# First pass of gated linear attention: second decay and exponential buffers, modulation work between key steps, keys made on VectorE

## The chip, the cores and the metric

One core of a Trainium2 chip. The metric is the device time of one execution in microseconds (us). TensorE multiplies matrices, VectorE and ScalarE work element by element (ScalarE with tables for exponential and logarithm), GpSimd (POOL in the rows) works element by element too and issues gathers, SyncE (SP) issues DMAs.

## What is computed

One layer of a trunk on 128 context tokens and 1024 latent tokens of width 1024, in float32. What matters here, from the reference:

```
m = silu(cond) @ w_ada + b_ada                       # six modulation rows per conditioning vector
h = rms_norm(x, norm_mix) * (1 + sc1) + sh1
la = log_sigmoid(lr @ w_gate + b_gate) / 16          # one decay per head, column and direction
# gated linear attention, both directions, 4 heads, keys of 64, values of 128:
cum = cumsum(la)
o = (q * exp(cum)) @ S  +  (scores of q, k with exp(cum_i - cum_j), masked) @ v
S = exp(last) * S + (k * exp(last - cum)).T @ v
# then attention over keys with cached context keys and values, the output projection,
# and a mixture of 32 experts on all tokens
```

## The kernel before, in words

The program is a row of stages. A stage is one block in which each engine has its own list of instructions, in order, with semaphores between the lists; the next stage begins when all five lists have ended. Tokens go in 9 tiles of 128 (tile 0 is the context, 1 to 8 the latents). The stages are: the first modulation rows; the input projection; gated linear attention (L595 to L990, the stage the change is in); softmax attention (from L1008); output projection and router; and the experts, which take most of the time.

The gated-linear-attention stage has two passes over the nine tiles, `for i in range(NT)` and then `for s in range(NT)`. The first pass takes tiles in the order `FIRST`. For step i, with g = FIRST[i]:

- `gates(i)` (PE, L884): decay logits of the tile, into one of four PSUM banks; issued four steps ahead. `size` (ACT, L676, L677) and `log` (ACT, L681): absolute value, exponential and logarithm; the logarithm needs another table than the exponential, so three tiles' logarithms go together (an ACT_TABLE_LOAD before and after).
- `decay(i)` (DVE, L794 to L806): log-sigmoid, cumulative sum along the tile, differences `Dt` against the tile's middle, and twelve small columns `vecs`.
- `grow(i)` (ACT, L687, L689, L690): `ek` and `eq`, the exponentials of minus and plus `Dt`, and that of the small columns.
- `decayed(i)` (POOL, L757, L760, L762): keys times `ek` for both directions (`kf`, 512 columns), then queries times `eq` for the backward direction (written over the keys) and for the forward one.
- `turn(i)` (PE, L893): four transposes of the decayed keys. `keep_turned(i)` (ACT, L695) copies them from PSUM. `sums(i)` (PE, L903): keys times values, the tile's part of the state. `add(i)` (DVE, L812) takes it to `UX`. `step(k)` (DVE, L822): one tile's state in one direction, sixteen in all.

Between these stands the work on the other modulation rows: eight pieces of `w_ada`, 2 MB each, in a ring of two buffers that SyncE fills (`load`, L629). `ada_part(n)` (PE, L913) multiplies a piece, `ada_keep(n)` (ACT, L700) copies the partial sums, `ada_sum(n)` (PE, L921, L922) adds them and the bias, `ada_row(n)` (ACT, L708) copies the row out, or `ada_scaled(n)` (DVE, L829) for pieces 4 and 5. `ADA_AT` says which steps have a piece (i = 1, 2, 4, 5, 7, 8), and `ADA_LATE` puts pieces 6 and 7 into the second pass. In the kernel before, TensorE's order in a step is gates, turn, sums, ada_sum of the last piece, ada_part of this one.

The second pass, tile g = SECOND[s]: `score` (PE, L931), `mask` (DVE, L835, L837), `centred` (POOL, L770), `mix` (PE, L947, L951), `square` (ACT, L714), `mean` and `gated` (DVE, L841, L848), and GpSimd's power at L781. SyncE's list, in order: constants and states, two modulation pieces, the zeroing of the experts' sums (L650, L652), the new states, then pieces and rows in turn, a piece's load waiting for the product that used its buffer last.

In the softmax-attention stage SyncE first issues the cached keys and values (L1013, L1014), and TensorE begins by transposing the cached keys (L1140), which waits for them; then come the scores of the context tile (L1145).

Of the kernel before, what the change touches and what calls it, by code (L numbers as in the profile page):

```python
# [16 lines left out]
P = 128  # L17
# [17 lines left out]
def trunk_kernel(nc, t_in, t_out):  # L35
# [52 lines left out]
    with ctx:  # L88
# [97 lines left out]
        pre, Dt, ek, eq, kTM, part = (ar(40320 + H * i, H) for i in range(6))  # L186
        nrow2 = ar(43392, H, 2)
        mrow2 = [ar(43904 + H * i, H, 2) for i in range(2)]
        brow2 = [ar(44928 + H * i, H, 1) for i in range(2)]
        sc = [[ar(45952 + 2 * H * i + H * half, H) for half in range(2)] for i in range(2)]  # L190
        sc_both = [ar(45952 + 2 * H * i, 2 * H) for i in range(2)]
        Sc = [r3(ar(48000 + H * i, H), 4) for i in range(2)]
        seen = ar(49024, H).bitcast(I32)
        zeros, osq = ar(49536, P), ar(50700, H)
        keep = ar(50180, H)
        scP = ar(49920, 32 * KT)
        sel = ar(50176, 2)
# [7 lines left out]
        kc = r3(ar(50816, NC * P), NC)  # L205
# [409 lines left out]
        with stage("pads_out") as block:  # L615
            @block.sync
            def _(sp):
# [41 lines left out]
                for n in range(2, NADA):  # L659
                    load(n)  # L660
                    row_out(n - 2)
                    rows(n)
                row_out(NADA - 2)
# [7 lines left out]
            def _(act):  # L671
# [11 lines left out]
                def grow(i):  # L683
                    g = FIRST[i]
                    act.wait_ge(sem("decay_made"), i + 1)
                    act.wait_ge(sem("kf_made"), i)
                    nc.scalar.activation(ek, Dt, ACT.Exp, scale=-1.0 / 16).then_inc(sem("ek_made"), 1)  # L687
                    act.wait_ge(sem("qf_made"), i)
                    nc.scalar.activation(eq, Dt, ACT.Exp, scale=1.0 / 16).then_inc(sem("eq_made"), 1)  # L689
# [31 lines left out]
                for i in range(NT):  # L721
                    if i % 3 == 0 and i + 3 < NT:
                        size(i + 3)
                        size(i + 4)
                    grow(i)
                    if i % 3 == 1 and i + 2 < NT:
                        size(i + 4)
                    keep_turned(i)
                    if i % 3 == 1 and i + 2 < NT:
                        for k in range(i + 2, i + 5):  # L730
                            log(k)
                    if i - 1 in ADA_AT:
                        ada_row(ADA_AT[i - 1])
                    if i in ADA_AT:
                        ada_keep(ADA_AT[i])
                ada_row(ADA_AT[NT - 1])
# [8 lines left out]
            def _(pool):  # L745
# [18 lines left out]
                def centred(s):  # L764
                    g = SECOND[s]
# [1240 lines left out]
```

## Time and profile before, and how to read it

| | |
|---|---|
| median of 3 runs | 2820.37 us (2819.17 to 2822.82) |
| the profiled execution | 2821.45 us, span 2819.8 us |
| busy over the span | PE 88%, DVE 58%, ACT 47%, POOL 30% |
| gated-linear-attention stage | about 419.7 to 584.5 us |
| its first pass, first to ninth transpose | 435.22 to 519.54 us |
| DMA | 539.95 MB, 191 GB/s over the span |

Times in rows are microseconds from the start of the span. A row of a timeline gives start, duration, engine, line, operation, result and source with their sizes, how many follow one another, and in brackets the engine's idle time before it and what ended it. PE is TensorE's matmul, PEld its weight load; a float32 product counts as two or more instructions. PEclk is the clock granted to TensorE, 1.00 for 2.4 GHz and 0.50 for 1.2 GHz.

### The profile page before, as it was taken

To read this page: it belongs to the slowest core of one execution; us is meant where nothing else is said; L and a number is where in the kernel's file an instruction comes from. 1 tells how busy PE (TensorE), PEld (TensorE's weight loads), DVE (VectorE), ACT (ScalarE), POOL (GpSimd) and SP (SyncE) were. 2 spreads that over 40 slices of the span, in tenths; PEclk is the share of its full clock that TensorE was granted. 3 is DMA by queue.
4 is the path that set the end of the run, shared out by engine and by line. 5 is a ranking of instruction groups with operands and counts; after the bars stand their busy time and mean duration, and the time that the engine had idled before them with its cause. 6 is when DMAs were issued, how large, how long until landed. Compare 5 with 4: busy or idle time off the path is not lost. (4 is left out here: it accounts for less than half of the span.)

```text
span 2819.8 us, 55873 instructions
## 1 busy us (share of the span) xinstructions
PE 2484.2 (88%) x19085; PEld 1367.2 (48%) x19086; DVE 1625.0 (58%) x1900; ACT 1322.4 (47%) x1351; POOL 833.6 (30%) x862
## 2 busy tenths in 40 slices
PE   4999986879999983989989999689998999998992
PEld 0555543456665542545545555345554455544551
DVE  1222215457774554595483567999869835256895
ACT  0111115235442223584482566888768725155771
POOL 3121122210000334333332343333344333233342
PEclk8999995789999986989989999899999999999996
DMA  8000007230003227787485678899979946158984
GB/s 329 27 9 17 17 6 241 91 109 1 0 0 121 90 83 259 228 326 280 119 327 173 204 243 289 329 398 394 368 257 369 356 128 209 30 147 291 340 305 151
DMA packets 176502, 539.95 MB, mean 191 GB/s; under 512 B 20644, under 2 KB 36438, under 8 KB 175380
## 3 DMA queue, kind: packets, MB, share of 16 engines
q1 hardware_dynamic: 146240, 488.92, 46.4%
q0 software_dynamic: 26720, 46.85, 7.7%
q10 hardware_dynamic: 3496, 3.61, 0.4%
q8 instruction: 24, 0.39, 0.1%
q14 instruction: 22, 0.18, 0.0%
HBM read 494.69 MB, written 45.21 MB: 191 GB/s over the span
## 5 line engine op out<-in xcount | busy, mean ns | idle before, releaser
L1910 PE MATMUL psum<-arena 128*64 128x512 bf16 x12528 | 1436.3, 386 | 98.9 <-DVE arena L1805 91.8
L1910 PEld LDWEIGHTS psum<-arena 128*64 128x64 bf16 x12528 | 727.2, 111 | 755.4 <-DVE arena L1805 115.8
L1805 DVE TENSOR_TENSOR arena<-arena 128x2048 bf16<-128x2048 f32 x384 | 858.1, 2285 | 179.8 <-ACT arena L1707 152.4
L1707 ACT ACTIVATE arena<-arena 128x2048 bf16<-128x2048 f32 x384 | 706.5, 1899 | 42.7 <-PE psum L1910 20.5
L1660 POOL DMA_INDIRECT expert_sums<-arena x90 | 186.3, 2071 | 540.2 <-issue 521.1
L559 PE MATMUL psum<-arena 128*128 128x512 f32 (+2 forms) x864 | 305.8, 511 | 1.2 <-issue 1.2
L1640 POOL DMA_INDIRECT arena<-expert_inputs,arena x88 | 130.1, 1478 | 484.7 <-DMA arena<-expert_lists 419.6
L559 PEld LDWEIGHTS psum<-arena 128*128 128x128 f32 x864 | 152.3, 193 | 133.1 <-issue 129.8
L1809 DVE TENSOR_TENSOR arena<-psum,arena 128x512 bf16<-128x512 f32 x87 | 59.6, 686 | 212.7 <-ACT arena L1717 212.7
L1728 ACT ACTIVATE arena<-psum,arena 128x512 f32<-128x512 f32 x87 | 59.7, 686 | 205.4 <-PE psum L1910 153.3
L1713 ACT ACTIVATE arena<-psum 128x1024 bf16<-128x1024 bf16 x87 | 88.5, 1018 | 125.1 <-PE psum L1910 118.7
L1671 POOL DMA_DIRECT2D arena<-expert_lists x174 | 130.2, 941 | 30.9 <-issue 25.6
L1723 ACT ACTIVATE arena<-arena 128x512 f32<-128x512 f32 x87 | 54.9, 631 | 174.0 <-DVE arena L1813 174.0
L1492 PE MATMUL psum<-arena 128*128 128x512 f32 x288 | 128.8, 601 | 1.4 <-DVE arena L1390 1.4
L1823 DVE TENSOR_SCALAR arena<-psum 128x512 f32<-128x512 f32 x87 | 59.9, 689 | 108.4 <-PE psum L1910 101.6
L1192 PE MATMUL psum<-arena 128*128 128x128 f32 x640 | 105.4, 288 | 6.1 <-ACT arena L1055 2.9
L1717 ACT ACTIVATE arena<-psum 128x512 bf16<-128x512 f32 x87 | 51.6, 593 | 122.6 <-PE psum L1894 122.1
L1899 PE MATMUL psum<-arena 128*64 128x512 bf16 x522 | 103.1, 390 | 3.4 <-DMA arena<-bias_parts 2.8
L1201 PE MATMUL psum<-arena 128*64 128x128 f32 x1280 | 96.8, 282 | 0.0
L1063 ACT ACTIVATE arena<-psum 128x512 f32<-128x512 f32 x64 | 38.1, 597 | 115.8 <-PE psum L1192 115.8
L1888 PE MATMUL psum<-arena 128*128 128x128 bf16 x704 | 54.5, 221 | 41.7 <-DMA arena<-expert_inputs,arena 41.7
L1043 ACT ACTIVATE arena<-psum,arena 128x1280 f32<-128x1280 f32 x64 | 85.0, 1328 | 8.5 <-DVE arena L1093 1.3
(246 smaller groups left out, 2294.5 us busy)
## 6 DMA issues: line engine op xcount, KB each, us to landing
arena<-in_w_gu SPq DMA_DIRECT2D x256, 1024.0 KB
arena<-in_w_down SPq DMA_DIRECT2D x128, 1024.0 KB, 6.7
arena<-in_w_ada SPq DMA_DIRECT2D x12, 2048.0 KB, 10.3
arena<-in_w_in SPq DMA_DIRECT2D x8, 1168.0 KB, 20.5
arena<-in_x_sample SPq DMA_DIRECT2D x16, 512.0 KB
arena<-mod_rows SPq DMA_DIRECT2D x12, 512.0 KB, 7.3
expert_sums<-arena SPq DMA_DIRECT2D x10, 512.0 KB, 6.2
expert_inputs<-arena SPq DMA_DIRECT2D x10, 512.0 KB, 2.8
```

The costliest lines, as they stand in the source:

```text
L559: last = nc.tensor.matmul(bank(bk, n, off), hT[b][:, j * P:(j + 1) * P], w_in[:, j, lo:lo + n], start=(j == 0), stop=(j == KT - 1))
L1192: last = nc.tensor.transpose(bank(t_bank(r - 1, i), P, at * P), pr[(r - 1) % 2][:, v * KEYS + k * P:v * KEYS + (k + 1) * P], ident)
L1201: last = nc.tensor.matmul(bank(O_BANK)[heads_rows(v), q * P:(q + 1) * P], va[:, 1 + k, v * HD:(v + 1) * HD], pT[r % 2][:, v * KEYS + k * P ...
L1492: last = nc.tensor.matmul(bank(a), mixT[b][:, j * P:(j + 1) * P], w_out[:, j, a * H:(a + 1) * H], start=(j == 0), stop=(j == KT - 1))
L1640: pool.indirect_dma_start(out=xg, out_offset=None, in_=h2_d, in_offset=bass.IndirectOffsetOnAxis(ap=listed.bitcast(U32)[:, 0:1], axis=0)). ...
L1660: pool.indirect_dma_start(out=moe_halves, out_offset=bass.IndirectOffsetOnAxis(ap=held.bitcast(U32)[:, 2 * DELAY:2 * DELAY + 1], axis=0), ...
L1671: pool.dma_start(listed[group(h), :], pairs[:, h, :]).then_inc(sem("listed_in"), 16)
L1707: nc.scalar.activation(w_hi[c], raw[c], ACT.Copy).then_inc(sem(f"hi_made{c}"), 1)
L1713: nc.scalar.activation(xT, bank(B_X).bitcast(BF), ACT.Copy).then_inc(sem("xT_made"), 1)
L1805: nc.vector.tensor_tensor(w_lo[c], raw[c], w_hi[c], ALU.subtract).then_inc(sem(f"lo_made{c}"), 1)
L1899: nc.tensor.matmul(bank(b)[group(g)], pickrow[:, (first + g) * UNIT:(first + g + 1) * UNIT], rows, start=True, stop=False)
L1910: last = nc.tensor.matmul(bank(b)[group(g)], parts[part][:, cols], w[:, kk, g * H:(g + 1) * H], start=False, stop=(k == KT - 1 and part == 1))
```

## The change

In five parts, of which the last moves work from the stage behind into this one:

- `Dt` and `ek` have two buffers each, by the parity of i. `decay(i)` waits for the exponential of two steps back instead of the last, `grow(i)` for the keys of two steps back. The arena's map is laid out anew for it.
- The keys times `ek` are made by VectorE (`decay_keys`), behind the decay of the next tile and ahead of the state add; `add` and `step` each stand one step later in VectorE's list.
- On TensorE `ada_part(n)` stands ahead of `turn(i)` and `ada_sum(n)` between `turn(i)` and `sums(i)` of the same step; `score(0)` stands ahead of the last `turn`. On ScalarE `grow(i)` comes first, then `size` and `log`, `ada_keep`, `keep_turned`, `ada_row`.
- `mask(0)` stands ahead of the last `add`, and GpSimd's `centred` waits for the small columns' exponential.
- The four DMAs of cached keys and values are issued in this stage, ahead of the last two modulation rows, to a new place for the keys.

```
-        pre, Dt, ek, eq, kTM, part = (ar(40320 + H * i, H) for i in range(6))
+        pre, eq, kTM, part = (ar(40320 + H * i, H) for i in range(4))
+        Dt, ek = ([ar(42368 + H * (2 * k + i), H) for i in range(2)] for k in range(2))
...
+                sp.wait_ge(sem("z_made"), NT)
+                for a in range(NC):
+                    sp.dma_start(kc[:, a, :], t_in["cache_k"]...).then_inc(sem("cache_in"), 16)
+                    sp.dma_start(va[:, NT + a, :], t_in["cache_v"]...).then_inc(sem("cache_in"), 16)
                 row_out(NADA - 2)
...
                 def grow(i):
-                    act.wait_ge(sem("kf_made"), i)
-                    nc.scalar.activation(ek, Dt, ACT.Exp, scale=-1.0 / 16).then_inc(sem("ek_made"), 1)
+                    if i >= 2:
+                        act.wait_ge(sem("kf_made"), i - 1)
+                    nc.scalar.activation(ek[i % 2], Dt[i % 2], ACT.Exp, scale=-1.0 / 16).then_inc(sem("ek_made"), 1)
                     act.wait_ge(sem("qf_made"), i)
...
                 for i in range(NT):
-                    if i % 3 == 0 and i + 3 < NT:
+                    grow(i)
+                    if i + 3 < NT and i % 3 == 0:
                         size(i + 3)
                         size(i + 4)
-                    grow(i)
-                    if i % 3 == 1 and i + 2 < NT:
+                    if i + 4 < NT and i % 3 == 1:
                         size(i + 4)
-                    keep_turned(i)
-                    if i % 3 == 1 and i + 2 < NT:
                         for k in range(i + 2, i + 5):
                             log(k)
-                    if i - 1 in ADA_AT:
-                        ada_row(ADA_AT[i - 1])
                     if i in ADA_AT:
                         ada_keep(ADA_AT[i])
-                ada_row(ADA_AT[NT - 1])
+                    keep_turned(i)
+                    if i in ADA_AT:
+                        ada_row(ADA_AT[i])
...
                 def decayed(i):
-                    pool.wait_ge(sem("ek_made"), i + 1)
-                    nc.gpsimd.tensor_tensor(r4(kf[:, g, :]), k_tile(g).unsqueeze(1).broadcast_to([P, 2, 2, P]), r4(ek), ALU.mult).then_inc(sem("kf_made"), 1)
...
                 def centred(s):
+                    pool.wait_ge(sem("vecs_made"), FIRST.index(g) + 1)
...
                 def decay(i):
-                    dve.wait_ge(sem("eq_made"), i)
+                    if i >= 2:
+                        dve.wait_ge(sem("eq_made"), i - 1)
...
+                def decay_keys(i):
+                    g = FIRST[i]
+                    dve.wait_ge(sem("ek_made"), i + 1)
+                    nc.vector.tensor_tensor(r4(kf[:, g, :]), k_tile(g).unsqueeze(1).broadcast_to([P, 2, 2, P]), r4(ek[i % 2]), ALU.mult).then_inc(sem("kf_made"), 1)
...
                 for i in range(NT):
                     if i + 1 < NT:
                         decay(i + 1)
-                    add(i)
-                    if i == 1:
+                    decay_keys(i)
+                    if i >= 1:
+                        add(i - 1)
+                    if i == 3:
                         dve.wait_ge(sem("state_in"), 64)
-                    if i >= 2:
-                        step(i - 2)
+                    if i >= 3:
+                        step(i - 3)
...
-                step(NT - 2)
                 dve.wait_ge(sem("sc_cleared"), 2)
                 dve.wait_ge(sem("seen_in"), 16)
                 mask(0)
-                for k in range(NT - 1, len(STEPS)):
+                step(NT - 3)
+                add(NT - 1)
+                for k in range(NT - 2, len(STEPS)):
                     step(k)
...
                     if i + 4 < NT:
                         gates(i + 4)
-                    turn(i)
-                    sums(i)
-                    if i - 1 in ADA_AT:
-                        ada_sum(ADA_AT[i - 1])
                     if i in ADA_AT:
                         ada_part(ADA_AT[i])
-                pe.wait_ge(sem("decay_logged"), NT)
-                score(0)
-                ada_sum(ADA_AT[NT - 1])
+                    if i == NT - 1:
+                        score(0)
+                    turn(i)
+                    if i in ADA_AT:
+                        ada_sum(ADA_AT[i])
+                    sums(i)
```

TensorE, steps i = 7 and 8 of the first pass and the begin of the second, before. L893 is a transpose group, L903 the state sums, L921 and L922 a modulation sum, L913 a modulation product, L931 a score group:

```order
L893 MATMUL psum<-arena 128x128 x4
L903 MATMUL psum<-arena 64x128 x8
L913 MATMUL psum<-arena 32x512 x8
L893 MATMUL psum<-arena 128x128 x4
L903 MATMUL psum<-arena 64x128 x8
L921 MATMUL psum<-arena 2x512
L922 MATMUL psum<-arena 2x512
L913 MATMUL psum<-arena 32x512 x8
L931 MATMUL psum<-arena 128x128 x8
L921 MATMUL psum<-arena 2x512
L922 MATMUL psum<-arena 2x512
L931 MATMUL psum<-arena 128x128 x8
```

The same two steps with the change, where L904 is the transpose group, L914 the state sums, L932 and L933 the modulation sum, L924 the product and L942 the score group:

```order
L924 MATMUL psum<-arena 32x512 x8
L904 MATMUL psum<-arena 128x128 x4
L932 MATMUL psum<-arena 2x512
L933 MATMUL psum<-arena 2x512
L914 MATMUL psum<-arena 64x128 x8
L924 MATMUL psum<-arena 32x512 x8
L942 MATMUL psum<-arena 128x128 x8
L904 MATMUL psum<-arena 128x128 x4
L932 MATMUL psum<-arena 2x512
L933 MATMUL psum<-arena 2x512
L914 MATMUL psum<-arena 64x128 x8
L942 MATMUL psum<-arena 128x128 x8
```

The product went from behind the step's state sums to ahead of its transposes, the modulation sum from the step after to between transposes and state sums, and the first score from behind the last product to ahead of the last transposes.

VectorE, step i = 3 of the first pass, before. L794 to L806 are the decay of tile i + 1, L812 the state add, L822 a state step:

```order
L794 SCALAR_TENSOR_TENSOR arena<-psum,arena 128x512
L796 SCALAR_TENSOR_TENSOR arena<-arena 128x512
L797 TENSOR_TENSOR arena<-arena 128x256
L800 TENSOR_TENSOR arena<-arena 128x256
...
L806 TENSOR_TENSOR arena<-arena 128x2
L812 TENSOR_TENSOR arena<-psum,arena 128x512
L822 SCALAR_TENSOR_TENSOR arena<-arena 128x128 x2
```

And with the change (L814 is the key product, L820 the add, L830 the step):

```order
L795 SCALAR_TENSOR_TENSOR arena<-psum,arena 128x512
L797 SCALAR_TENSOR_TENSOR arena<-arena 128x512
L798 TENSOR_TENSOR arena<-arena 128x256
L803 TENSOR_TENSOR arena<-arena 128x256
...
L809 TENSOR_TENSOR arena<-arena 128x2
L814 TENSOR_TENSOR arena<-arena 128x512
L820 TENSOR_TENSOR arena<-psum,arena 128x512
L830 SCALAR_TENSOR_TENSOR arena<-arena 128x128 x2
```

The key product is new on VectorE, between the next tile's decay and the add, and the add is now that of the step before.

## Rows read from the trace of the kernel before

**Rows 1.** Busy time by stretch: PE, PEld, DVE, ACT, POOL, then PEclk, DMA share, GB/s.

```profile
435.20:477.40 42.20, 32.09 (x152) 16.47 (x152) 22.81 (x50) 17.65 (x32) 11.94 (x12) 0.58 0.83 262
477.40:519.50 42.10, 27.62 (x136) 11.44 (x136) 21.88 (x49) 15.06 (x28) 11.13 (x12) 0.62 0.29 101
...
536.40:584.50 48.10, 41.57 (x408) 31.54 (x408) 22.10 (x70) 12.45 (x76) 17.20 (x23) 1.00 0.08 30
```

**Rows 2.** Waits from 434 to 530 (us in total, times, longest).

```profile
POOL arena L757 <- ACT arena L687: 71.1, 9, 12.1
...
PE psum L893 <- POOL arena L757: 22.7, 8, 4.0
```

**Rows 3.** Timeline of TensorE, step i = 5 and the next transposes.

```profile
487.69 1.12 PE L893 MATMUL psum<-arena 128*128 128x128 f32 x4 [4.01 <-POOL arena L757]
489.49 1.98 PE L903 MATMUL psum<-arena 128*64 128x128 f32 x16 [0.69 <-ACT arena L695]
...
494.05 3.30 PE L913 MATMUL psum<-arena 128*32 128x512 f32 x13
499.95 0.90 PE L893 MATMUL psum<-arena 128*128 128x128 f32 x3 [2.60 <-POOL arena L757]
```

**Rows 4.** Timelines of ScalarE and GpSimd, the same stretch.

```profile
495.09 0.59 ACT L708 ACTIVATE arena<-psum 2x512 f32<-2x512 f32 x1 [5.65 <-PE psum L922]
...
497.93 0.62 ACT L687 ACTIVATE arena<-arena 128x512 f32<-128x512 f32 x1
...
498.63 1.27 POOL L757 TENSOR_TENSOR arena<-arena 128x512 f32<-128x512 f32 x1 [9.26 <-ACT arena L687]
```

**Rows 5.** Timeline of TensorE, first, fifth and ninth transposes of the pass.

```profile
435.22 1.11 PE L893 MATMUL psum<-arena 128*128 128x128 f32 x4 [3.65 <-POOL arena L757]
...
477.42 1.12 PE L893 MATMUL psum<-arena 128*128 128x128 f32 x4 [0.54 <-POOL arena L757]
...
519.54 0.74 PE L893 MATMUL psum<-arena 128*128 128x128 f32 x4 [2.59 <-POOL arena L757]
```

**Rows 6.** Timeline of VectorE, a decay's begin, the next one's, and an add.

```profile
428.69 0.69 DVE L794 SCALAR_TENSOR_TENSOR arena<-psum,arena 128x512 f32<-128x512 f32 x1 [13.61 <-ACT arena L681]
...
432.17 0.68 DVE L794 SCALAR_TENSOR_TENSOR arena<-psum,arena 128x512 f32<-128x512 f32 x1
...
491.51 0.69 DVE L812 TENSOR_TENSOR arena<-psum,arena 128x512 f32<-128x512 f32 x1 [1.84 <-PE psum L903]
```

**Rows 7.** Timeline of TensorE at either clock, and busy time of one stretch.

```profile
438.92 2.07 PE L884 MATMUL psum<-arena 33*128 33x128 f32 x8
...
532.06 1.02 PE L922 MATMUL psum<-arena 128*2 128x512 f32 x2
...
542.24 1.92 PE L913 MATMUL psum<-arena 128*32 128x512 f32 x16
...
516.50:520.00 3.50, 0.91 (x8) 0.42 (x4) 0.00 (x0) 1.75 (x4) 1.64 (x2) 0.99 0.00 0
```

**Rows 8.** Timeline of VectorE, from the first mask to the second.

```profile
532.62 3.23 DVE L822 SCALAR_TENSOR_TENSOR arena<-arena 128x128 f32<-128x128 f32 x12
...
536.42 1.31 DVE L837 COPY_PREDICATED arena<-arena,psum 128x512 f32<-128x512 int32 x2
```

**Rows 9.** One line's instructions, ns min/median/max, first and last start.

```profile
L800 DVE TENSOR_TENSOR arena<-arena x9: 424/1000/1006, 431.1 to 509.1; 128x256 f32<-128x256 f32 x9
```

**Rows 10.** Timeline of SyncE's queue, and DMA issues from 455 to 475.

```profile
456.59 0.59 SPq L629 DMA_DIRECT2D arena<-in_w_ada  x1
...
arena<-in_w_ada SPq DMA_DIRECT2D x2, 2048.0 KB, 7.8
```

**Rows 11.** Timeline, begin of the softmax-attention stage.

```profile
588.10 0.36 SPq L1013 DMA_DIRECT2D arena<-in_cache_k  x1
...
591.33 0.69 PE L1140 MATMUL psum<-arena 128*128 128x128 f32 x2 [10.46 <-DMA arena<-in_cache_v]
```

**Rows 12.** The page's DMA issues (KB each, median us to landing).

```profile
arena<-in_w_in SPq DMA_DIRECT2D x8, 1168.0 KB, 20.5
```

More of the change, by code:

```diff
@@ L185, in trunk_kernel @@
         RING_B = [r3(ar(32128 + 4096 * i, 4096), KT) for i in range(2)]
-        pre, Dt, ek, eq, kTM, part = (ar(40320 + H * i, H) for i in range(6))
[L187 to L197, printed above, removed]
+        pre, eq, kTM, part = (ar(40320 + H * i, H) for i in range(4))
+        Dt, ek = ([ar(42368 + H * (2 * k + i), H) for i in range(2)] for k in range(2))
+        nrow2 = ar(44416, H, 2)
+        mrow2 = [ar(44928 + H * i, H, 2) for i in range(2)]
+        brow2 = [ar(45952 + H * i, H, 1) for i in range(2)]
+        sc = [[ar(46976 + 2 * H * i + H * half, H) for half in range(2)] for i in range(2)]
+        sc_both = [ar(46976 + 2 * H * i, 2 * H) for i in range(2)]
+        Sc = [r3(ar(49024 + H * i, H), 4) for i in range(2)]
+        seen = ar(50048, H).bitcast(I32)
+        zeros, scP, sel, keep = ar(50560, P), ar(50688, 32 * KT), ar(50944, 2), ar(50948, H)
+        osq = ar(40320, H)
         oattT = r3(ar(36224, 4 * TOK), 4)
@@ L204, in trunk_kernel @@
         mx3, mx2, c_sum, c_share = ar(25472, 3), ar(25475, 2), ar(25477, NH), ar(25485, NH)
-        kc = r3(ar(50816, NC * P), NC)
+        kc = r3(ar(51460, NC * P), NC)
         w_out = r3(ar(27008, KT * DM), KT)
@@ L613, in trunk_kernel @@
         u4 = lambda ap: ap.rearrange("p (u t) -> p u t", u=4)
-        with stage("pads_out") as block:
+        with stage("pads_out cache_in") as block:
             @block.sync
@@ L662, in _ @@
                     rows(n)
+                sp.wait_ge(sem("z_made"), NT)
+                for a in range(NC):
+                    sp.dma_start(kc[:, a, :], t_in["cache_k"][0, 0, a * P:(a + 1) * P].rearrange("s h d -> s (h d)")).then_inc(sem("cache_in"), 16)
+                    sp.dma_start(va[:, NT + a, :], t_in["cache_v"][0, 0, a * P:(a + 1) * P].rearrange("s h d -> s (h d)")).then_inc(sem("cache_in"), 16)
                 row_out(NADA - 2)
@@ L685, in grow @@
                     act.wait_ge(sem("decay_made"), i + 1)
-                    act.wait_ge(sem("kf_made"), i)
-                    nc.scalar.activation(ek, Dt, ACT.Exp, scale=-1.0 / 16).then_inc(sem("ek_made"), 1)
+                    if i >= 2:
+                        act.wait_ge(sem("kf_made"), i - 1)
+                    nc.scalar.activation(ek[i % 2], Dt[i % 2], ACT.Exp, scale=-1.0 / 16).then_inc(sem("ek_made"), 1)
                     act.wait_ge(sem("qf_made"), i)
-                    nc.scalar.activation(eq, Dt, ACT.Exp, scale=1.0 / 16).then_inc(sem("eq_made"), 1)
+                    nc.scalar.activation(eq, Dt[i % 2], ACT.Exp, scale=1.0 / 16).then_inc(sem("eq_made"), 1)
                     nc.scalar.activation(vecs[:, :, :, g], vecs[:, :, :, g], ACT.Exp, scale=1.0 / 16).then_inc(sem("vecs_made"), 1)
@@ L798, in decay @@
                     last, c_f, c_b = col(p4, P - 1), col(p4[:, 0:2], mid - 1), col(l4[:, 2:4], mid)
-                    dve.wait_ge(sem("eq_made"), i)
-                    nc.vector.tensor_tensor(r4(Dt)[:, 0], p4[:, 0:2], bc(c_f, P), ALU.subtract)
-                    nc.vector.tensor_tensor(r4(Dt)[:, 1], bc(c_b, P), l4[:, 2:4], ALU.subtract)
+                    if i >= 2:
+                        dve.wait_ge(sem("eq_made"), i - 1)
+                    to = r4(Dt[i % 2])
+                    nc.vector.tensor_tensor(to[:, 0], p4[:, 0:2], bc(c_f, P), ALU.subtract)
+                    nc.vector.tensor_tensor(to[:, 1], bc(c_b, P), l4[:, 2:4], ALU.subtract)
                     nc.vector.tensor_copy(vecs[:, 0, :, g], last)
@@ L1010, in _ @@
             def _(sp):
-                for a in range(NC):
-                    sp.dma_start(kc[:, a, :], t_in["cache_k"][0, 0, a * P:(a + 1) * P].rearrange("s h d -> s (h d)")).then_inc(sem("cache_in"), 16)
-                    sp.dma_start(va[:, NT + a, :], t_in["cache_v"][0, 0, a * P:(a + 1) * P].rearrange("s h d -> s (h d)")).then_inc(sem("cache_in"), 16)
                 for c in range(2):
```

## The prediction

> **What bounds the kernel now.** I read the busy times by stretch first. The gated-linear-attention stage is 165 us of 2820. In its first pass, the first two rows of [rows 1], TensorE works 59.7 of 84.3 us and no other engine more than 44.7: no engine is full, so the order of waits sets the time. The granted clock there is 0.58 and 0.62, so the 1.2 GHz level for most of the stretch; in the second pass, the third row, it is 1.00. The waits [rows 2] say who is late: GpSimd waits 71.1 us for ScalarE's exponential, TensorE 22.7 us for GpSimd's keys.
>
> The period from i = 5 to 6 shows the ring [rows 3, 4]. TensorE transposes the keys (487.69), multiplies them into the state sums (489.49), does the modulation sum, which ScalarE takes at 495.09, and the next modulation product (until 497.35). Only then does ScalarE copy that, form the exponential (497.93), and GpSimd multiply the keys (498.63); the next transpose starts at 499.95. The period is 12.26 us, and TensorE idles 2.6 us in front of the transpose. Every modulation piece stands in the ring whole, because ScalarE forms step i+1's exponential behind step i's modulation copy. From the first transpose (435.22) to the ninth (519.54) are 84.3 us [rows 5], 10.5 a period.
>
> **The change, part by part.** (a) *Keys on VectorE.* GpSimd's product takes 1.27 us [rows 4]; the VectorE product of 512 columns nearest to it takes 0.69 (L812) [rows 6]: 0.6 us less in the ring, nine more instructions (about 6 us) on VectorE, which has room. Against it: the first key product now stands behind the second tile's decay. The decay occupies VectorE 3.5 us undisturbed (428.69 to the next at 432.17) [rows 6], so the first product starts at about 435.7; GpSimd's 1.27 us before the transpose at 435.2 began at 433.9; the first transpose moves to about 436.5: +1.3 us.
>
> (b) *Second decay and exponential buffers.* They let the decay and the exponential run a tile ahead. Alone they are worth little: in the period shown the exponential waits for ScalarE's own turn behind the modulation work, not for a buffer. Late next is GpSimd's query product, which the second exponential still waits for; it is 1.5 us a step and hidden. Cost of the buffers themselves: nothing, they are addresses.
>
> (c) *The modulation product ahead of the transpose, the modulation sum ahead of the state sums.* The product needs only weights that have landed, so it runs while ScalarE and VectorE make the keys; the state sums and the next product then run behind the modulation row that ScalarE waits for. The ring that is left is exponential 0.6, keys 0.7, transpose 1.1, modulation sum 3.6, row copy 0.6: 6.9 us with hand-offs at the low clock [rows 3, 4]. TensorE's own list becomes the longer one. Between first and ninth transpose it holds 8 transposes, 8 state sums, 5 modulation sums, 6 products, 4 gate groups and one score. At 1.2 GHz [rows 3, 4, 7]: 8x1.12 + 8x1.98 + 5x3.6 (from the state sums' end to 495.09) + 6x3.3 + 4x2.07 + 2.0 (the score has as many matmuls as the state sums) = 72.9 us. At 2.4 GHz [rows 5, 7]: 8x0.74 + 8x1.2 + 5x2.04 (L921 as L922) + 6x1.92 + 4x1.2 + 1.2 = 43 us. State sums, gates and score at that level have no row here; half their length and all of it bound them, and I take 1.2, nearer to the half, since products and sums go from 3.3 to 1.92 and from 3.6 to 2.04. At the high level VectorE is the longer: 3.5 decay + 0.69 keys + 0.69 add + 0.54 step = 5.4 us a step [rows 6, 8].
>
> (d) *GpSimd beside VectorE.* L800 takes 424 ns alone and 1000 in most steps [rows 9], and it stands in the list where GpSimd multiplies. Before, GpSimd worked 2.8 us a step (11.94 and 11.13 us in four steps each [rows 1]), and L800 alone lost 0.58. Now it works 1.5 us a step, beginning with the add, which reads PSUM, so I take 0.5 to 0.9 us: 5.9 to 6.3 us a step. The Trainium skill ("SBUF — State Buffer", Who interferes with whom) states that a VectorE instruction with two SBUF inputs contends with GpSimd's reads, and one with a single SBUF input does not. The new key product has two SBUF inputs; by that rule it meets only GpSimd's products of the step before, which are over.
>
> (e) *Which clock.* In the trace the clock is at 2.4 GHz right behind a full modulation product, 0.99 at 516.5 to 520.0 [rows 7]. There it is wasted, since TensorE works 0.91 of those 3.5 us. Now transpose and sums stand right behind the product. I take the high level for most of the last half, and one period of four at the low one: one at 1.12 + 1.98 + 3.6 + 3.3 = 10.0, three at 6.3, 7.2 us a period. The Trainium skill ("TensorE: Matmul & The Clock Gate", What's actually happening) says that activity releases the throttle and idling brings it back; the second pass, busy 41.6 of 48.1 us at 1.00 [rows 1], agrees.
>
> (f) *Weights.* The third piece (2 MB) is issued at 456.6, behind the zeroing of the expert sums, and lands 7.8 us later, at 464.4 [rows 10]. The change doesn't move that issue. The fifth transpose (tile step i = 4) now stands behind its product, so it can't start before 464.4 + 1.9; with most of the product at the low clock I take 467.5, against 477.42 [rows 5]. TensorE's list up to that point (4 transposes, 4 state sums, 2 modulation sums, 3 products, 4 gate groups) would end at 436.5 + 37.8 = 474 all low and 459 all high, so 467.5 is also its middle: -9.9 us, with the +1.3 of (a) and ScalarE's logarithm groups of i = 1 and i = 4 inside it (the second runs while the piece is waited for). Pieces 3, 4 and 5 are issued two pieces ahead, some 15 us, and hidden; without that cover each costs up to what a landing exceeds it by.
>
> (g) *Last four periods.* Before 519.54 - 477.42 = 42.1 us, now 4x7.2 = 28.8: -13.3 us.
>
> (h) *End of the first pass.* From the ninth transpose to the second mask (L837, 536.42) were 16.9 us [rows 5, 8]: modulation sum, last product, score and sum stood in between. Now product and score are in front. Left are transpose 0.74, sum 2.0, state sums 1.2, hand-offs 0.2, add 0.6, nine steps of two instructions at 0.27 us (12 took 3.23 [rows 8]) 4.9, scaling 0.6: 10.2 us, so -6.7 us. From there the second pass is as before; its two products have their weights 10 us earlier.
>
> (i) *Cached keys and values.* Now the attention stage issues them at 588.10 and TensorE starts at 591.33 [rows 11]. Issued a stage earlier, TensorE can start at about 588.2: -3.1 us. The four issues (1.6 us of the queue) stand in front of the last two rows, whose sources come much later: nothing.
>
> Sum: -9.9 - 13.3 - 6.7 - 3.1 = -33.0 us. The profiled execution took 2821.45 us (span 2819.8), so 2788.4 for its like; the median of the runs is 2820.37, 1.1 lower: **2787.4 us**. The fast end takes 466.3 in (f), 6.0 a period and 9.8 in (h): -11.1 - 18.1 - 7.1 - 3.1 = -39.4, 2781.0. Later stages lie behind this one and shift with it.
>
> **Rivals.** *The clock stays at 1.2 GHz.* For it: the mean is 0.58 and 0.62 in the first pass [rows 1]. Against it: every full product raised it. Then 436.5 + 72.9 = 509.4 for the ninth transpose, 13.0 us behind it (1.12, 3.6 and 1.98 in (h)): 522.4 against 536.4, with (i) -17.1 us: 2803.3.
>
> *Weights come late.* TensorE now stands still for a late piece before it transposes. If a landing takes 20.5 us, as w_in's do [rows 12], the third piece costs 12.7 us: 2800.1. Against it: 7.8 us in this very stretch.
>
> *VectorE becomes the bound, slower than before.* If GpSimd's lock held all of VectorE's step at L800's ratio, 1.00/0.424 = 2.36, the 5.4 us would be 12.7 a period: +17 us over eight, the nine late steps 6.6 more, which eats (h), with (i) +14: 2834. It decides from some 10.9 us a period, twice the undisturbed 5.4. Against it: GpSimd works only 1.5 us a step.
>
> *The gain is given back.* The second pass waits for the last two modulation rows or pieces, and a few us remain: 2817. Nothing in its rows shows such a wait.
>
> **How the numbers follow.** Forecast 0.68 (2780 to 2797), clock low 0.19, weights late 0.06, given back 0.03, lock 0.04. A measurement tells 0.2% (5.6 us) from no change. Faster by more takes the first three: 0.93; within 0.03; slower 0.04. The range 2780 to 2806 holds the forecast and the low clock with 2 us of slack, and leaves out the ends.
>
> **What would show it.** Transposes some 7 us apart with the fifth near 467; the second mask near 504; granted clock over 0.8 in the last half of the pass; GpSimd's products 1.5 us a step; L800's like mostly 0.42 us; no wait of TensorE at the attention stage's start. It is wrong if TensorE waits for weights after the third piece, if the clock stays at 0.5, or if periods stay over 9 us.

## The result and the profile after

| | us |
|---|---|
| before, median of 4 runs (the three above and one beside the change) | 2820.30 (2819.17 to 2822.82) |
| after, median of 4 runs | 2780.57 (2778.91 to 2782.44) |
| ratio | 0.9858, 95% interval 0.9841 to 0.9875 |
| profiled execution, before and after | 2821.45, 2780.45 (span 2778.8) |

The kernel got faster by 1.4%, 39.7 us between the medians, where -33.0 was forecast. The time 2780.57 lies just inside the range, 0.6 us above its low end; that it fell inside is in part luck, since four executions of the same kernel later ran from 2777.10 to 2783.32 (experiment 12).

The stretches come first, with the columns of [rows 1]: first to fifth transpose, fifth to ninth, second pass.

```profile
434.90:468.80 33.90, 27.85 (x168) 14.45 (x168) 24.44 (x57) 21.07 (x37) 8.07 (x10) 0.70 1.00 315
468.80:493.30 24.50, 20.81 (x160) 8.64 (x156) 17.37 (x44) 11.78 (x23) 5.81 (x8) 0.93 0.49 174
502.00:549.00 47.00, 41.56 (x408) 31.54 (x408) 21.02 (x67) 11.53 (x69) 17.16 (x23) 1.00 0.10 33
```

The two halves took 42.2 and 42.1 us and take 33.9 and 24.5. The granted clock rose from 0.58 and 0.62 to 0.70 and 0.93. The second pass is what it was. The waits from 434 to 502 answer to [rows 2]:

```profile
POOL arena L760 <- DVE arena L814: 55.6, 9, 14.3
...
PE psum L904 <- DVE arena L814: 7.6, 3, 4.8
DVE arena L814 <- ACT arena L691: 7.3, 3, 4.6
```

TensorE waits 7.6 us for keys instead of 22.7. GpSimd's 55.6 us of waiting cost nothing. Below, TensorE from the third modulation piece on (i = 4 to 7), to be read beside [rows 3]:

```profile
465.54 3.40 PE L924 MATMUL psum<-arena 128*32 128x512 f32 x16 [2.78 <-DMA arena<-in_w_ada]
468.87 0.66 PE L904 MATMUL psum<-arena 128*128 128x128 f32 x4
469.66 1.02 PE L932 MATMUL psum<-arena 1*2 1x512 f32 x2
470.61 1.02 PE L933 MATMUL psum<-arena 128*2 128x512 f32 x2
471.56 1.09 PE L914 MATMUL psum<-arena 128*64 128x128 f32 x16
472.58 1.92 PE L924 MATMUL psum<-arena 128*32 128x512 f32 x16
474.97 0.66 PE L904 MATMUL psum<-arena 128*128 128x128 f32 x4 [0.47 <-DVE arena L814]
...
480.86 0.66 PE L904 MATMUL psum<-arena 128*128 128x128 f32 x4 [2.31 <-DVE arena L814]
482.20 1.98 PE L914 MATMUL psum<-arena 128*64 128x128 f32 x16 [0.69 <-ACT arena L699]
484.11 2.65 PE L924 MATMUL psum<-arena 128*32 128x512 f32 x16
486.75 0.66 PE L904 MATMUL psum<-arena 128*128 128x128 f32 x4
```

From 465.54 to 474.50 product, transposes, modulation sum, state sums and the next product stand almost without a gap. At 2.4 GHz each takes little over half of its time at the low level in [rows 3, 7]. The periods from fifth to ninth transpose are 6.10, 5.89, 5.89 and 6.60 us. At 480.86 TensorE has waited 2.31 us for VectorE's keys, so its own work doesn't set that period. VectorE has no gap in the next, in which the clock fell for the state sums (1.98):

```profile
474.23 0.69 DVE L814 TENSOR_TENSOR arena<-arena 128x512 f32<-128x512 f32 x1 [4.64 <-ACT arena L691]
...
480.12 0.68 DVE L814 TENSOR_TENSOR arena<-arena 128x512 f32<-128x512 f32 x1
480.72 0.68 DVE L820 TENSOR_TENSOR arena<-psum,arena 128x512 f32<-128x512 f32 x1
481.32 1.30 DVE L830 SCALAR_TENSOR_TENSOR arena<-arena 128x128 f32<-128x128 f32 x2
482.55 0.68 DVE L795 SCALAR_TENSOR_TENSOR arena<-psum,arena 128x512 f32<-128x512 f32 x1
...
486.01 0.68 DVE L814 TENSOR_TENSOR arena<-arena 128x512 f32<-128x512 f32 x1
```

From one key product to the next are 5.89 us: VectorE is the bound there. That holds for the two periods of 5.89 us. In the first of the four (6.10) VectorE's key product, at 474.23, waited 4.64 us for ScalarE's exponential, which stood behind the modulation row's copy and a table load. In the last (6.60) TensorE's list, now with the first score in it, has no gap over 0.1 us from 486.75 to 493.35.

**Where the 41.0 us of the profiled pair are.** I count from the stage's first decay (428.69 before, 427.29 after), so that what lies ahead of the stage drops out:

| us after the first decay | before | after | difference, of this stretch alone |
|---|---|---|---|
| first transpose | 6.53 | 7.68 | +1.15 |
| fifth transpose | 48.73 | 41.58 | -8.30 |
| ninth transpose | 90.85 | 66.06 | -17.64 |
| second mask | 107.73 | 74.75 | -8.19 |
| last gated output of the second pass | 154.69 | 121.69 | -0.02 |
| attention's first transpose | 162.64 | 126.45 | -3.19 |

That makes -36.2. The stage itself began 1.4 us earlier, and the experts' long stretch (first to last start of its main product, L1916 after) took 1672.5 us instead of 1676.4. The change touches neither. The other runs show that the latter is chance (experiment 12), and the stage's first decay stood anywhere from 425.4 to 427.2 us in the twelve kernels run later, so it too varies. Half a microsecond the other way is spread over the rest. What the prediction said would show it is there: transposes 7.3 us apart on the mean, the fifth at 468.87, the second mask at 502.04, the clock over 0.8 in the last half, and no wait for weights after the third piece.

### The profile page after: what moved, and what is told of

The parts are those of the page before. It is cut to its first block and busy times, and to the rows that moved or that the text cites. A ratio compares the mean times of both kernels' runs of the same rounds, so it can differ in the third digit from the quotient of the medians.

```text
span 2778.8 us, 55870 instructions
## 1 busy us (share of the span) xinstructions
PE 2464.0 (89%) x19085; PEld 1360.0 (49%) x19086; DVE 1621.5 (58%) x1909; ACT 1321.6 (48%) x1351; POOL 816.8 (29%) x853
## 5 line engine op out<-in xcount | busy, mean ns | idle before, releaser
L1916 PE MATMUL psum<-arena 128*64 128x512 bf16 x12528 | 1437.2, 386 | 94.6 <-DVE arena L1811 89.1
L1916 PEld LDWEIGHTS psum<-arena 128*64 128x64 bf16 x12528 | 728.3, 112 | 750.6 <-DVE arena L1811 111.6
L1713 ACT ACTIVATE arena<-arena 128x2048 bf16<-128x2048 f32 x384 | 706.4, 1898 | 42.2 <-PE psum L1916 20.0
L1646 POOL DMA_INDIRECT arena<-expert_inputs,arena x88 | 139.0, 1580 | 493.4 <-DMA arena<-expert_lists 427.7
```

What stands on the lines that cost most here:

```text
L1646: pool.indirect_dma_start(out=xg, out_offset=None, in_=h2_d, in_offset=bass.IndirectOffsetOnAxis(ap=listed.bitcast(U32)[:, 0:1], axis=0)). ...
L1713: nc.scalar.activation(w_hi[c], raw[c], ACT.Copy).then_inc(sem(f"hi_made{c}"), 1)
L1916: last = nc.tensor.matmul(bank(b)[group(g)], parts[part][:, cols], w[:, kk, g * H:(g + 1) * H], start=False, stop=(k == KT - 1 and part == 1))
```

## The experiments

"Second mask" below is its time after the first decay: before 107.7, after 74.8 (73.0 when the same kernel ran again, so that a difference of under 2 us there tells nothing). A ratio is to the kernel before, run beside it on the same chip, with its 95% interval; where neither stands, the kernel ran once. Line numbers shift by a line or two between the kernels, so parts go by their names.

**1. The old order with everything else of the change.** TensorE and ScalarE lists as before; keys on VectorE, two buffers and the early cached keys stay.

```
-                    if i in ADA_AT:
-                        ada_part(ADA_AT[i])
                     turn(i)
-                    if i in ADA_AT:
-                        ada_sum(ADA_AT[i])
                     sums(i)
+                    if i - 1 in ADA_AT:
+                        ada_sum(ADA_AT[i - 1])
+                    if i in ADA_AT:
+                        ada_part(ADA_AT[i])
```

> The changed kernel, with the order of the modulation work on TensorE and ScalarE put back as it was before; keys on VectorE, two buffers and the early cached keys stay. If the order makes the gain, the ring keeps every modulation piece: it is shorter than before only by the faster key product (0.6 us in each of 8 periods) and the cached keys (3.2 us), so some 8 us below before, 2812. If keys on VectorE or the buffers make the gain, it stays near the changed kernel, 2781 to 2790.

Measured 2817.67 us (ratio 0.9992, 0.9981 to 1.0002); second mask 106.45. The order carries the gain. Keys, buffers and cache together are not told from nothing in the median, and the 1.3 us at the second mask are less than the same kernel varies by. The trace does have the 3.2 us at the attention stage.

**2. The order alone.** Keys on GpSimd, one buffer, add and step in their old places; new order, early cache.

```
                 def grow(i):
-                    if i >= 2:
-                        act.wait_ge(sem("kf_made"), i - 1)
+                    act.wait_ge(sem("kf_made"), i)
...
                 def decayed(i):
+                    pool.wait_ge(sem("ek_made"), i + 1)
+                    nc.gpsimd.tensor_tensor(r4(kf[:, g, :]), ..., r4(ek[0]), ALU.mult).then_inc(sem("kf_made"), 1)
...
-                    decay_keys(i)
-                    if i >= 1:
-                        add(i - 1)
+                    add(i)
```

> The new order of the modulation work alone (with the early cached keys): keys on GpSimd, one decay and one exponential buffer, adds and steps as before. If the order makes the gain, most of it is here: periods of some 7 to 8 us, 2790. If keys and buffers make it, near 2815.

Measured 2782.27 us (0.9869, 0.9853 to 0.9886); second mask 76.43. The intervals of this ratio and of the change's overlap: new order and early cache give all that can be told.

**3. Keys on GpSimd, two buffers.** `decay_keys` is taken out and the product put back on GpSimd.

> The changed kernel with the key product back on GpSimd (1.27 us instead of 0.69). VectorE bounds the late periods at 5.9 us if the trace is read right; it loses an instruction of 0.6 us and meets GpSimd for 2.8 us a step instead of 1.5, so both sides weigh about the same: 2781 to 2786. If the key product in the ring bounds, 0.6 us in each of 8 periods: 2785.5. If keys on VectorE were what makes the gain, over 2800.

Measured 2782.49 us (0.9871, 0.9852 to 0.9889); second mask 74.26. Moving the keys to VectorE is worth nothing that can be told: it takes 0.6 us out of the hand-off and puts as much into the engine that bounds the late periods.

**4. One buffer.** `Dt` and `ek` single, the waits one step tighter, all else as after.

```
-                    if i >= 2:
-                        dve.wait_ge(sem("eq_made"), i - 1)
+                    dve.wait_ge(sem("eq_made"), i)
```

> The changed kernel with one decay and one exponential buffer. VectorE then waits with each decay's differences until the second exponential of the step before is made, and the key product stands behind that decay: ring of exponentials 1.1, differences and small columns 1.3, keys 0.7, transpose and sum 2.7, row 0.6, 6.4 us a period instead of 5.9 in the late ones and some 1 to 2 us more in the early ones: 2784 to 2790. If the buffers are worth nothing, 2781.

Measured 2785.91 us (0.9879, 0.9862 to 0.9895); second mask 76.90. The longest of its waits that the kernel after does not have, from 434 to 502, is the decay's for the exponential that still reads `Dt`:

```profile
DVE arena L801 <- ACT arena L692: 11.0, 5, 4.3
```

The mask comes 2.2 us later than in the change, 3.9 later than in experiment 12, so its own size is not well known. The four late periods tell more: they sum to 27.1 us, against 24.5 and 24.6 in two executions of the change, so the second buffers are worth 2.6 us there. Up to the fourth transposes another 2.8 us are lost (31.73 us after the first decay for 28.93), but these fall into the wait for the third piece. With keys on GpSimd the two kernels (experiments 2 and 3, mask 76.43 and 74.26) differ in the order of add, step and mask as well, and only 0.5 us of the difference lies in the late periods.

**5. Cached keys late.** The four DMAs back in the attention stage.

> The changed kernel with the four DMAs of cached keys and values back at the start of the attention stage. If TensorE's wait there was the whole of term (i), the stage's first transpose comes 3.2 us later behind the second pass's end (8.0 us instead of 4.8) and nothing else moves: 2783.8. If the first score waits for another engine in either case, no difference.

One run: 2785.13 us. From the last gated output to attention's first transpose are 7.95 us, as before, against 4.76 with the change: 3.2 us, the forecast's 3.1.

**6. The experts' sums zeroed late.** The zeroing DMAs go behind the last piece, so that the third piece is not queued behind them.

```
                 load(0)
                 load(1)
-                sp.wait_ge(sem("zeroed"), 1)
-                for a in range(NT + 1):
-                    sp.dma_start(moe_d[a * P:(a + 1) * P, :]...).then_inc(sem("zeros_out"), 16)
```

> The changed kernel with the zeroing of the expert sums (11 DMAs, 5.8 MB written) issued behind the last modulation piece, in the second pass, where the DMA engines idle. If the third piece's landing held the fifth transpose, the 2.8 us of TensorE's wait go, less what ScalarE's logarithm group then sets (it ends at 467.0, the product would at 466.2): 2 to 3.5 us less in the period of 12.65, 2778. If the logarithm group was the bound in any case, 0 to 0.5 us. If the zeroing is missed later or collides with pieces 6 and 7, slower by some us.

Measured 2785.02 us (0.9873, 0.9856 to 0.9889); second mask 73.38. The wait for the piece is gone (the product starts at 462.58 with no idle time), but the next wait stood right behind it:

```profile
467.46 1.02 PE L932 MATMUL psum<-arena 1*2 1x512 f32 x2 [1.20 <-ACT arena L704]
468.40 1.87 PE L933 MATMUL psum<-arena 128*2 128x512 f32 x2
470.20 1.87 PE L914 MATMUL psum<-arena 128*64 128x128 f32 x16
```

ScalarE copies the partial sums only behind a table load and three logarithms (until 466.9), TensorE waits, and the clock falls during the sums. The next period grew from 6.1 to 8.24 us. Of 3.1 us in the one period 1.4 were left at the mask, no more than the same kernel varies by, and nothing at the end of the second pass (121.91 us after the first decay for 121.69). The 2778 expected did not come. A version with the logarithms elsewhere was not tried; none of the kernels run beats the change.

**7. Keys made twice.** VectorE makes each step's key product once more, into a place nobody reads.

> The changed kernel with a second key product per step on VectorE (into unused space, 0.6 us, ahead of the one that counts). If VectorE bounds the periods from the sixth transpose on, each of these grows from 5.9 to 6.5, and where it doesn't bound nothing: 3 to 5 periods, +2 to +3 us in the pass. If TensorE's list bounds, +0 in those periods.

One run: 2781.94 us; second mask 75.32. The key products of two steps stand 6.49 us apart:

```profile
478.62 0.69 DVE L814 TENSOR_TENSOR arena<-arena 128x512 f32<-128x512 f32 x1
479.22 0.69 DVE L815 TENSOR_TENSOR arena<-arena 128x512 f32<-128x512 f32 x1
...
485.11 0.69 DVE L814 TENSOR_TENSOR arena<-arena 128x512 f32<-128x512 f32 x1
```

5.89 plus 0.60 is 6.49: in the two periods that took 5.89 us VectorE's list is the bound, to a hundredth. The last late period did not grow (6.45 us for 6.60): that one is TensorE's. Up to the fourth transposes the extra work shows too (30.36 us after the first decay for 28.93) and then falls into the wait for the third piece. At the mask the expected +2 to +3 us are 0.6 against the change and 2.4 against its second execution (experiment 12), too uncertain to count.

**8. Each modulation product of the first pass twice.**

> The changed kernel with each of the six modulation products of the first pass made twice on TensorE (same result, 1.92 us at the high clock, 3.4 at the low). TensorE's list in a late period is 0.66 + 2.0 + 1.1 + 1.9 = 5.7 of 5.9 us, so nearly all of it should show: 1.7 us in each late step with a piece, more in the first one: +9 to +12 us in the pass, 2791. If the order of waits bounds and TensorE has slack, under +3.

One run: 2786.98 us; second mask 80.17, 5.4 later (7.2 later than in experiment 12). That lies between the two cases expected. The extra product is 1.7 to 3.0 us of TensorE in each of six steps, some 12 us in all, of which about half is hidden beside the other engines. TensorE has slack beside VectorE, but less than a product.

**9. Only the product ahead of the transposes.** From the kernel after, the modulation sum put behind the state sums.

```
                     turn(i)
+                    sums(i)
                     if i in ADA_AT:
                         ada_sum(ADA_AT[i])
-                    sums(i)
```

> The kernel after, with TensorE's modulation sum put behind the state sums of the same step; the product stays ahead of the transposes, ScalarE's order is the new one. Theory A (the product's place carries the gain, since before it ended last in each step and ScalarE's copy of it stood ahead of the next exponential): the row copy now comes one state sum (1.1 to 2.0 us) later, hidden in part under VectorE's 5.9 us a step; second mask 76 to 80 us after the first decay (74.8 in the kernel after), 2782 to 2788 us. Theory B (the sum has to be ahead of the state sums as well, since ScalarE takes the row before the next exponential): the late periods go to 8 us, second mask 82 to 90, 2789 to 2797 us.

Measured 2786.45 us (0.9883, 0.9867 to 0.9900); second mask 79.00. Both lie in theory A's ranges: with the product ahead and ScalarE's new order, 27.4 of the 31.7 us between experiment 1 and the change are there at the mask, and the sum's place ahead of the state sums adds 4.3. ScalarE's order alone can't be run with TensorE's old one: ScalarE would wait for the product ahead of copying the transposes, and TensorE would wait for that copy ahead of the product.

**10. Only the modulation sum ahead of the state sums.** From experiment 1, the sum of the step before between transposes and state sums; the product stays last.

> The kernel with the old order of modulation work on TensorE and ScalarE, and in it only the modulation sum of the step before moved ahead of the state sums; the product stays last in its step. Theory A (the product's place carries the gain): the ring over the product stays as it was, the row copy only starts 1.1 to 2.0 us earlier while the product behind it still ends last; second mask 103 to 107 us after the first decay (106.5 in the old order), 2813 to 2818 us. Theory B (half of the gain is the sum's): second mask 88 to 98, 2797 to 2808 us.

Measured 2802.10 us (0.9937, 0.9920 to 0.9953); second mask 95.87. Theory A had 103 to 107, theory B 88 to 98: it is B, and theory A falls in this form. The shares of the two moves don't add up (10.6 us for the sum alone here, 4.3 on top of the product in experiment 9), so neither has one price.

**11. TensorE's new order, ScalarE's old one.**

```
                 for i in range(NT):
-                    grow(i)
...
                     keep_turned(i)
...
+                    if i - 1 in ADA_AT:
+                        ada_row(ADA_AT[i - 1])
                     if i in ADA_AT:
                         ada_keep(ADA_AT[i])
-                    keep_turned(i)
-                    if i in ADA_AT:
-                        ada_row(ADA_AT[i])
```

> The kernel after on TensorE, with ScalarE's old order: transposes' copy before the copy of the partial sums, the row copied a step later. Theory A (TensorE's place of the product carries the gain, ScalarE's order little): the modulation sum waits for the transposes' copy and that of the partial sums one behind the other, some 1 us more in a step with a piece, and TensorE has about that slack; second mask 75 to 80 us after the first decay, 2781 to 2788 us. Theory C (ScalarE's order is needed too): TensorE stands still 1.5 us or more in each of the six steps with a piece, second mask 84 to 90, 2790 to 2797 us.

Measured 2802.55 us (0.9938, 0.9921 to 0.9955); second mask 94.40. Theory C, and more: TensorE waits for the copy of the partial sums, which now stands behind the copy of the transposes:

```profile
PE psum L934 <- ACT arena L704: 13.9, 6, 4.1
```

**The orders side by side.** The stretch from first to ninth transpose, with the columns of [rows 1]: experiment 1 (old order), 10 (sum moved), 11 (ScalarE's order old), 9 (sum behind), and after.

```profile
433.04:512.79 79.75, 59.28 (x288) 27.77 (x288) 40.24 (x96) 32.58 (x59) 12.41 (x16) 0.60 0.58 187
```

```profile
433.72:506.43 72.71, 54.64 (x289) 25.59 (x289) 40.07 (x96) 32.58 (x59) 12.40 (x16) 0.68 0.63 205
```

```profile
434.28:511.06 76.78, 58.23 (x324) 26.48 (x324) 40.21 (x99) 31.87 (x59) 13.88 (x18) 0.69 0.60 194
```

```profile
433.07:496.81 63.74, 52.16 (x324) 23.84 (x324) 42.53 (x99) 32.60 (x60) 13.90 (x18) 0.77 0.73 235
```

```profile
434.97:493.35 58.38, 48.71 (x324) 23.09 (x325) 41.74 (x99) 32.85 (x60) 13.88 (x18) 0.80 0.78 255
```

Those with x324 hold 36 instructions more: a product (1.92 us), a score (1.16) and a modulation sum (2.04), which now stand ahead of the ninth transposes. Less those 5.1 us, TensorE's busy time for the same instructions goes from 59.3 (old order) to 43.6 us (after): 15.7 us are the clock. Its idle time (stretch less busy) goes from 20.5 to 9.7: 10.8 us are waits. Experiment 10 shows how both hang together, in the period that [rows 3] show of before:

```profile
481.15 1.11 PE L906 MATMUL psum<-arena 128*128 128x128 f32 x4 [3.40 <-DVE arena L816]
482.20 1.86 PE L934 MATMUL psum<-arena 1*2 1x512 f32 x2
483.99 1.87 PE L935 MATMUL psum<-arena 128*2 128x512 f32 x2
485.79 1.81 PE L916 MATMUL psum<-arena 128*64 128x128 f32 x16
487.53 1.92 PE L926 MATMUL psum<-arena 128*32 128x512 f32 x16
491.41 0.65 PE L906 MATMUL psum<-arena 128*128 128x128 f32 x4 [1.96 <-DVE arena L816]
```

The product still ends last and the ring is the same, yet the period is 10.26 us instead of 12.23 in experiment 1. From the transposes' start to the product's end are 8.3 us; there they were 10.25 (483.22 to 493.47). The modulation sum fills the 0.69 us in which TensorE waited for ScalarE's copy of the transposes, and the product that follows runs at 2.4 GHz, 1.92 us for all 16 instructions, where [rows 3] show 3.30 for 13 of them. That the filled gap is what raised the clock is argued from these rows; no run filled it with idle work alone. Such a gap doesn't always come with the low level: in experiments 11 and 12 state sums behind a gap of 0.69 us took 1.09 us, the time at 2.4 GHz (at 496.29 and at 479.27).

**12. The kernel after, once more.**

> The kernel after once more, to see what varies between builds and executions of the same code. If the 3.9 us by which the experts' stage of the profiled execution after was shorter than before is chance, this one's experts' stage lies anywhere in 1672 to 1680 us (the eight kernels so far span 1672.5 to 1679.3), and its median in 2778 to 2787 us; if the change brings it, the stage is 1672.5 within 0.5 us. Second mask at 74.8 within 0.3 us after the first decay either way.

Measured 2782.27 us (2777.10 to 2783.32; 0.9868, 0.9851 to 0.9884). The experts' stretch took 1674.7 us, and the stage's first decay stood at 426.00. Over all the kernels here, whose code there is the same, it took 1672.5 to 1679.3, so the 3.9 us of the first pair are chance. I expected the second mask within 0.3 us of 74.8, and it came at 72.97: the product on the third piece started at 36.1 us after the first decay instead of 38.3, since the piece landed 8.4 us behind its issue and not 10.2. The second pass took 48.5 us instead of 46.9 and gave most of that back, see the last section.

## Why the prediction was right

The direction and the mechanism held. The sum was 3.2 us short up to the attention stage's first transpose (-36.2 for -33.0): two terms were too small by 4.3 and 1.5 us, and one was too large by 2.8, so errors cancelled in part. What lies outside, mostly chance, added the rest.

- **(a)** held. First transpose +1.15 us, forecast +1.3; the product takes 0.68. But it brings nothing on the whole (experiment 3).
- **(b)** "They are worth little" held for the old order (experiment 1); the sum gave them nothing in the new one as well, and there it was wrong by 2 us or more (experiment 4). Once the wait for ScalarE's turn was gone, the buffer's came up.
- **(c)** The order is the gain: experiments 1 and 2. What I had not priced apart is ScalarE's half. With TensorE's new order alone (experiment 11) 20 us are lost. And I took the gain for one of who waits for whom, with the clock as an extra; by experiment 10 a third of it (10.6 of 31.7 us at the second mask) comes with the product still last in its step.
- **(d)** held where VectorE is the bound, in two of the four late periods: 5.89 us, forecast 5.9 to 6.3. The price fell on other instructions: the decay's L803, which is L800 of [rows 9], is now undisturbed, and the two instructions of the state step take 1.30 us instead of 0.60, +0.70.

```profile
L803 DVE TENSOR_TENSOR arena<-arena x9: 424/424/426, 429.7 to 485.0; 128x256 f32<-128x256 f32 x9
```

- **(e)** is the step that failed most. I charged one late period of four at the low clock, 10.0 us. There was one such stretch (the state sums at 482.20 took 1.98, the product 2.65), and it cost nothing, since VectorE was the bound of that period. The four took 6.10, 5.89, 5.89 and 6.60 us, 6.1 on the mean for the 7.2 forecast. Besides, the 3.3 us taken for a product at the low level, here and in the rival of the low clock, is 13 of its 16 instructions in [rows 3]; a whole one took 3.64 us at 440.68.
- **(g)** is the sum of it: -17.64 for -13.3.
- **(f)** was too large: -7.15 for -9.9 (-9.04 in experiment 12). "The change doesn't move that issue" was true of the third piece, 28.0 us after the first decay in both. But the fourth piece was issued 6.1 us behind it before (462.70) and now 1.4 us behind it (456.69), because the product that frees its buffer ends sooner; the two 2 MB loads now overlap. The issues at 455.25 and at 456.69:

```profile
arena<-in_w_ada SPq DMA_DIRECT2D x1, 2048.0 KB, 10.2
...
arena<-in_w_ada SPq DMA_DIRECT2D x1, 2048.0 KB, 14.0
```

  The landing took 10.2 us and not 7.8, which is most of the 2.8 us missing. It is the weak form of the rival *Weights come late*; experiment 6, with the piece there in time, ended the second pass no sooner. That the fourth load held the third up is not shown. In the nine runs that issue the two 1.4 us apart the third took 8.2 to 10.2 us, and with the fourth 4.7 us or more behind it 7.9 to 8.3 (before, experiments 1, 10 and 11). But pieces 6 and 7, issued 1.2 us apart in the second pass of the kernel after, took 7.8 and 13.3: there the first of the pair lost nothing.
- **(h)** -8.19 for -6.7. Behind the last add stood seven state steps (3.76 us for 14 instructions), not nine (4.9 us). The loop that ends the pass does run from the eighth step to the last, but `STEPS` has seven pairs, fourteen steps and not the sixteen counted at the head of this document.
- **(i)** held: -3.19 for -3.1; TensorE starts behind the stage's boundary and waits for no DMA.

```profile
553.74 0.66 PE L1146 MATMUL psum<-arena 128*128 128x128 f32 x2 [7.26 <-PEq L107]
```

Of the rivals, *the clock stays at 1.2 GHz* didn't come: 0.80 over the pass. *VectorE becomes the bound* came, but at 5.89 us and not at 10.9. *The gain is given back* didn't: the second pass takes 47.0 us in both.

By the Trainium skill ("SBUF — State Buffer", Who interferes with whom), cited in (d), a VectorE instruction with two SBUF inputs contends with a GpSimd instruction that reads SBUF, and one with a single SBUF input does not. The trace agrees: the add, one of whose inputs is in PSUM, keeps its 0.68 us at 480.72 while GpSimd starts a product at 480.95, and the state step behind it, with SBUF inputs alone, takes 1.30 us for 0.60.

## What to carry to other kernels

When one engine works on two jobs, put what another engine waits for early and fill the hand-offs with the second job, and reorder the lists of both engines together: TensorE's new order without ScalarE's gave 15 of 37 us. A gap can cost more than its length: of the 26.5 us that the same work got shorter between the first and the ninth transposes, 15.7 are a higher clock and 10.8 shorter waits. And where a faster loop frees a buffer sooner, ask beside which transfer the next load will now run: the second of two loads issued 1.4 us apart landed after 14.0 us for 7.7 before. Here it was still early enough.

## What was not expected of the hardware

- The same kernel's second pass took 46.9 us in one execution and 48.5 in another. In the slower, TensorE's score behind the 2.63 us of idling before the second pass ran at the low level: 1.77 us for 1.16, and the next two rows too (1.13 for 0.64, 1.74 for 1.16). First the kernel after, then experiment 12:

```profile
503.49 1.16 PE L942 MATMUL psum<-arena 64*128 64x128 f32 x16 [2.63 <-DVE arena L845]
```

```profile
500.42 1.77 PE L942 MATMUL psum<-arena 64*128 64x128 f32 x16 [2.63 <-DVE arena L845]
```

  The idling is as long in both, and the clock fell in one and not in the other. So it is with the state sums behind the fourth transposes: behind 1.90 us of idling in either execution they took 1.98 us at 458.78 and 1.09 at 457.48. Experiment 6 met the lower level ahead of its second pass too (1.62 us, second pass 48.5). Differences of under 2 us between kernels with such a gap say nothing in one execution.
- Where VectorE's state step meets GpSimd's products, VectorE pays alone, 0.70 us a step: GpSimd's first product of a step takes 724 to 734 ns in all nine steps, and its second 0.72 to 0.73 us in eight. Once GpSimd paid: the second product at 435.90, beside VectorE's scan, took 1522 ns.
- Of two loads of 2 MB issued 1.4 us apart the second pays for certain: 12.4 to 14.0 us in nine runs, for 7.7 to 7.9 where they stand 5 us or more apart (before and after). The first took anything from 8.2 to 10.2, and what decides this stays open.
